# Inverse of the long convolution: plain float32 products become three products of split operands

## The reference, cut to what matters

```python
n = 2 * L                                     # L = 512 tokens
y = jnp.fft.irfft(jnp.fft.rfft(s, n=n, axis=1) * jnp.fft.rfft(g, n=n, axis=0)[None], n=n, axis=1)[:, :L]
y = (y + s * skip.astype(jnp.float32)).astype(u.dtype) * x0
return y @ w_out + b_out
```

## Time and profile before

| | us |
|---|---|
| median of 3 runs (1364.06 to 1364.46) | 1364.25 |
| the profiled execution: its own time | 1364.25 |
| the profiled execution: its span | 1362.4 |
| TensorE busy | 1350.7 (99%) |
| VectorE busy | 993.7 (73%) |
| ScalarE busy | 637.4 (47%) |
| GpSimd busy | 122.0 (9%) |

### The profile page before, as it was taken

One profiled execution on the slowest core, in us unless ns is written; L12 is line 12 of the kernel. 1 busy time (PEld: TensorE's weight loads), 2 busy tenths in 40 slices (PEclk: granted clock), 3 DMA queues, 4 the chain that ended last, 5 costly groups with the idle time before them and its releaser, 6 DMA issues.

```text
span 1362.4 us, 18513 instructions
## 1 busy us (share of the span) xinstructions
PE 1350.7 (99%) x7232; PEld 1142.9 (84%) x7232; DVE 993.7 (73%) x1348; ACT 637.4 (47%) x901; POOL 122.0 (9%) x143
## 2 busy tenths in 40 slices
PE   9999999999999999999999999999999999999997
PEld 7777887888788889888898888878888899889986
DVE  7767788555666997865886786777878689548844
ACT  6546686333444454542564554533344445325532
POOL 1010157000000000000001221024000000000000
PEclk9999999999999999999999999999999999999999
DMA  7222345422112323223232223341223332322321
GB/s 276 98 98 78 125 145 195 156 79 76 63 62 93 113 103 124 94 93 105 99 107 84 102 93 100 107 160 36 93 93 108 108 124 94 124 93 93 109 77 62
DMA packets 28166, 144.50 MB, mean 106 GB/s; under 512 B 3210, under 2 KB 8611, under 8 KB 13496
## 3 DMA queue, kind: packets, MB, share of 16 engines
q1 hardware_dynamic: 24744, 133.97, 28.7%
q0 software_dynamic: 2656, 8.72, 1.8%
q10 hardware_dynamic: 688, 0.73, 0.2%
HBM read 136.84 MB, written 6.30 MB: 105 GB/s over the span
## 4 chain that ended last, share of the span: by engine, by line
PE 94%; DVE 2%; ACT 1%; DMA 1%; issue 1%; SPq 0%; POOL 0%; DVEq 0%; ACTq 0%
PE ps L2198 28%; PE ps L2200 28%; PE ps L2199 28%; PE ps L2614 1%; PE ps L2416 1%; PE ps L2429 1%; PE ps L2564 1%; PE ps L2406 1%; PE ps L2455 1%; PE ps L2802 1%; PE ps L2800 1%; PE ps L2806 1%; PE ps L2456 0%; PE ps L2457 0%; DMA f_out<-f_out_dram 0%
## 5 line engine op out<-in xcount | busy, mean ns | idle before, releaser
L2198 PE MATMUL ps<-opA_hi,w_hi 128*128 128x512 f32 (+1 forms) x944 | 353.6, 375 | 0.7 <-DVE w_lo L1346 0.4
L2200 PE MATMUL ps<-opA_hi,w_lo 128*128 128x512 f32 (+1 forms) x944 | 349.4, 370 | 0.0
L2199 PE MATMUL ps<-opA_lo,w_hi 128*128 128x512 f32 (+1 forms) x944 | 349.1, 370 | 0.0
L1346 DVE TENSOR_TENSOR w_lo<-raw,w_hi 128x2048 fp32r<-128x2048 f32 x112 | 256.5, 2291 | 77.5 <-ACT w_hi L747 76.2
L747 ACT CAST w_hi<-raw 128x2048 fp32r<-128x2048 f32 x111 | 211.6, 1907 | 190.3 <-PE ps L2200 183.7
L2198 PE MATMUL ps<-opB_hi,w_hi 128*128 128x512 f32 (+1 forms) x584 | 226.8, 388 | 1.7 <-DVE opB_lo L1382 1.0
L2199 PE MATMUL ps<-opB_lo,w_hi 128*128 128x512 f32 (+1 forms) x584 | 225.8, 387 | 0.0
L2200 PE MATMUL ps<-opB_hi,w_lo 128*128 128x512 f32 (+1 forms) x584 | 225.8, 387 | 0.0
L2198 PEld LDWEIGHTS ps<-opA_hi,w_hi 128*128 128x128 f32 x944 | 178.2, 189 | 32.4 <-issue 1.7
L2200 PEld LDWEIGHTS ps<-opA_hi,w_lo 128*128 128x128 f32 x944 | 178.0, 189 | 30.5
L2199 PEld LDWEIGHTS ps<-opA_lo,w_hi 128*128 128x128 f32 x944 | 178.2, 189 | 29.2 <-issue 0.2
(11 more groups left out here) (457 smaller groups left out, 2142.7 us busy)
## 6 DMA issues: line engine op xcount, KB each, us to landing
raw<-weights_dram SPq DMA_DIRECT2D x113, 1024.0 KB, 4.9
g_dram<-g_stage POOLq DMA_DIRECT2D x8, 512.0 KB, 3.0
h<-x_t_dram SPq DMA_DIRECT2D x7, 512.0 KB, 7.0
g_spec<-g_dram SPq DMA_DIRECT2D x5, 512.0 KB, 4.1
scores<-g_dram SPq DMA_DIRECT2D x3, 512.0 KB, 5.3
out_dram<-h SPq DMA_DIRECT2D x6, 256.0 KB, 2.3
mem_raw<-mem_t_dram POOLq DMA_DIRECT2D x1, 1024.0 KB, 8.4
c_keys<-c_dram POOLq DMA_DIRECT2D x4, 256.0 KB, 3.7
```

The source lines that it names most:

```text
L1346: V.tensor_tensor(w_lo[:, p, :], raw[:, p, :], w_hi[:, p, :].bitcast(F32), ALU.subtract).then_inc(lo_ready, 1)
L2198: W.matmul(out, w[0], x[0], start=start, stop=False, skip_group_check=mixed)
L2199: W.matmul(out, w[0], x[1], start=False, stop=False, skip_group_check=mixed)
L2200: return W.matmul(out, w[1], x[0], start=False, stop=stop, skip_group_check=mixed)
```

## The change

The inverse works on split operands. The parts of `y_spec` are made per pair of tiles: `spectrum_hi(half, q)` on ScalarE and `spectrum_lo(half, q)` on VectorE, 128x1024 each, the low part in the place of `y_spec` itself, the high part of half 0 in both slots of `raw` and of half 1 in the place of the products `spec`. `inv` is padded to even column counts (258, 256), ScalarE writes zeros into the pads, and it is split once: high parts into `w_hi[1]` and `inv_hi_es`, low parts in the place of `inv`. TensorE makes three passes where it made one float32 product. The Nyquist rows are copies of the parts, both on ScalarE. As `raw` is taken, both output weight pairs are loaded after `inv_done` 4. Their splits move to other places in both orders. The diff, cut:

```diff
@@ SP
-            sp.wait_ge(lo_ready, F_PAIR)
-            sp.dma_start(raw[:, 1, :], a["weights"][in_dram(I_PAIR + 2)]).then_inc(raw_in[1], 16)
...
-            sp.wait_ge(lo_ready, F_PAIR + 1)
-            sp.dma_start(raw[:, 0, :], a["weights"][in_dram(I_PAIR + 1)]).then_inc(raw_in[0], 16)
             for n in range(3, 8):
                 sp.wait_ge(fs_read, n - 2)
                 load_spectrum(n)
+            for p in range(2):
+                sp.wait_ge(inv_done, 4)
+                sp.dma_start(raw[:, p, :], a["weights"][in_dram(I_PAIR + 1 + p)]).then_inc(raw_in[p], 16)
@@ ScalarE
+            def inv_split_hi():
+                act.wait_ge(inv_patched, 4)
+                A.copy(inv_hi[:], inv[:, 0:ES]).then_inc(inv_patched, 1)
+                act.wait_ge(nyq_row_made, 2)
+                A.copy(inv_hi_es[:], inv[:, ES:]).then_inc(hi_ready, 1)
+            def spectrum_hi(half, q):
+                act.wait_ge(spec_sum, 8 * half + 2 * q + 2)
+                if q == 0:
+                    act.wait_ge(row_zero, 2 * half + 2)
+                A.copy(y_hi[half][:, 2 * q:2 * q + 2, :], y_spec[half][:, 2 * q:2 * q + 2, :]).then_inc(y_hi_made, 1)
...
             row_zero_products(0)
+            act.wait_ge(lo_ready, F_PAIR + 1)
+            spectrum_hi(0, 0)
             inv_patch()
...
+            act.wait_ge(chunk_done, 2 * F_PAIR)
+            inv_split_hi()
+            for q in range(1, 4):
+                spectrum_hi(0, q)
             row_zero_products(1)
-            nyquist_hi(0)
-            nyquist_hi(1)
-            split_after(F_PAIR)
-            split_after(I_PAIR)
-            for c in range(KT):
+            nyquist_rows(0)
+            act.wait_ge(spec_sum, 14)
+            spectrum_hi(1, 0)
+            spectrum_hi(1, 1)
+            even_part(0)
+            act.wait_ge(spec_sum, 16)
+            spectrum_hi(1, 2)
+            spectrum_hi(1, 3)
+            nyquist_rows(1)
+            even_part(1)
+            hyena_out_hi(0)
+            for c in range(2, KT):
                 even_part(c)
-                if c:
-                    hyena_out_hi(c - 1)
+                if c == 4:
+                    split_after(F_PAIR)
+                elif c == KT - 1:
+                    split_after(I_PAIR)
+                hyena_out_hi(c - 1)
@@ VectorE
+            def spectrum_lo(half, q):
+                dve.wait_ge(y_hi_made, 4 * half + q + 1)
+                tiles = slice(2 * q, 2 * q + 2)
+                lo_part(y_lo[half][:, tiles, :], y_spec[half][:, tiles, :], y_hi[half][:, tiles, :]).then_inc(y_lo_made, 1)
             for n in range(8):
-                if n == 7:
-                    nyquist_lo(0)
                 spectrum_products(n)
-            nyquist_lo(1)
+                if n in (2, 4):
+                    spectrum_lo(0, n // 2 - 1)
+                elif n == 3:
+                    dve.wait_ge(hi_ready, I_PAIR + 1)
+                    S.link(lo_part(inv_lo[:, EC:OS], inv[:, EC:OS], inv_hi[:, EC:OS]))
+                    S.link(lo_part(inv_lo[:, ES:], inv[:, ES:], inv_hi_es[:]))
+                elif n == 5:
+                    lo_part(inv_lo[:, OS:ES], inv[:, OS:ES], inv_hi[:, OS:ES]).then_inc(lo_ready, 1)
+                elif n == 6:
+                    spectrum_lo(0, 2)
+            spectrum_lo(0, 3)
+            spectrum_lo(1, 0)
+            spectrum_lo(1, 1)
             V.engine_nop().then_inc(bank_read, 4)
             for c in range(KT):
+                hyena_value(c)
+                if c == 0:
+                    spectrum_lo(1, 2)
+                    spectrum_lo(1, 3)
+                    continue
+                if c == 5:
+                    split_after(I_PAIR)
+                hyena_out_lo(c - 1)
                 if c == 4:
                     split_after(F_PAIR)
-                hyena_value(c)
-                if c:
-                    hyena_out_lo(c - 1)
-                if c == 6:
-                    dve.wait_ge(inv_done, 8)
-                    split_after(I_PAIR)
@@ TensorE, inverse(half)
                         if c == 0:
-                            pe.wait_ge(spec_sum, 8 * half + 2 * q + 2)
+                            pe.wait_ge(y_lo_made, Y_LO_BASE + 4 * half + q + 1)
...
+                        if q < 2:
+                            last = passes(bank[:, HALF - 2:T], y_re, columns(EC + q * (HALF + 2), HALF + 2), q == 0, False, mixed=True)
...
+                            passes(bank[:, 0:HALF], y_im, columns(ES + q * HALF, HALF, back=True), False, False, mixed=True)
                         else:
+                            passes(bank[:, 0:HALF], y_re, columns(OC + (q - 2) * HALF, HALF, back=True), False, False, mixed=True)
+                            passes(bank[:, HALF:T], y_im, columns(OS + (q - 2) * HALF, HALF), False, False, mixed=True)
@@ TensorE, before inverse(0)
-            pe.wait_ge(inv_patched, 1)
-            pe.wait_ge(hi_ready, I_PAIR + 1)
+            pair_ready(I_PAIR)
```

More of the change, by code:

```diff
@@ L135, in program @@
         w_lo = at("w_lo", [P, 2, 2 * CHUNK], F32R, 112 * KB)
[L137 removed]
+        inv, inv_lo = at("inv", [P, INV_COLS], F32, 120 * KB), at("inv_lo", [P, INV_COLS], F32R, 120 * KB)
+        inv_hi = at("inv_hi", [P, ES], F32R, 104 * KB)
         y_spec = [at("y_spec0", [P, KT, T], F32, 16 * KB), at("y_spec1", [P, KT, T], F32, 32 * KB)]
[L139 removed]
+        y_lo = [at("y_lo0", [P, KT, T], F32R, 16 * KB), at("y_lo1", [P, KT, T], F32R, 32 * KB)]
+        o = 128 * KB + 32
         vecs = at("vecs", [P, VECS], F32, o); o += 4 * ((VECS + 7) // 8 * 8)
@@ L752, in split_after @@
                     split_hi((g + 2) // 2, g % 2, past_fold=g + 2 > I_PAIR,
-                             used={F_PAIR: (fs_done, 8), I_PAIR: (chunk_done, 2 * F_PAIR)}.get(g))
+                             used={F_PAIR: (fs_done, 8), I_PAIR: (inv_done, 8)}.get(g))
             def root(i, width=T):
@@ L1200, in inv_patch @@
                 act.wait_ge(inv_in, 64)
-                A.activation(inv[0:1, ES:ES + P], ones[0:1, :], ACT.Copy, scale=0.0).then_inc(inv_patched, 1)
-                A.activation(inv[0:1, ES + P:ES + HALF - 1], ones[0:1, 0:P - 1], ACT.Copy, scale=0.0).then_inc(hi_ready, 1)
+                for cols in (slice(EC, OS, HALF + 2), slice(ES, INV_COLS, HALF)):
+                    A.activation(inv[:, cols], ones[:, 0:2], ACT.Copy, scale=0.0).then_inc(inv_patched, 1)
+                A.activation(inv[0:1, ES + 1:ES + 1 + P], ones[0:1, :], ACT.Copy, scale=0.0).then_inc(inv_patched, 1)
+                A.activation(inv[0:1, ES + 1 + P:ES + HALF], ones[0:1, 0:P - 1], ACT.Copy, scale=0.0).then_inc(inv_patched, 1)
+            def inv_split_hi():
[8 more added lines that the diff above has]
+                A.copy(y_hi[half][:, 2 * q:2 * q + 2, :], y_spec[half][:, 2 * q:2 * q + 2, :]).then_inc(y_hi_made, 1)
             def hy_taps(i, p):
@@ L1248, in hyena_out_hi, with nyquist_rows @@
                 A.copy(op_hi[1][:, c, :], hy_val_feat[:, c % 4, :]).then_inc(u_hi, 1)
-            def nyquist_hi(half):
+            def nyquist_rows(half):
                 act.wait_ge(nyq_cleared, 8 + half)
-                act.wait_ge(row_zero, 2 * half + 2)
-                A.copy(y_nyq[half][0:1, :], y_spec[half][0:1, 1, :]).then_inc(y_nyq_hi, 1)
+                act.wait_ge(y_hi_made, 4 * half + 1)
+                A.copy(y_nyq[half][0:1, :], y_hi[half][0:1, 1, :]).then_inc(y_nyq_lo, 1)
+                act.wait_ge(y_lo_made, Y_LO_BASE + 4 * half + 1)
+                A.copy(y_nyq[half][32:33, :], y_lo[half][0:1, 1, :]).then_inc(y_nyq_lo, 1)
             row_zero_products(0)
+            act.wait_ge(lo_ready, F_PAIR + 1)
+            spectrum_hi(0, 0)
             inv_patch()
@@ L2774, in inverse, with columns @@
             def inverse(half):
-                y = y_spec[half]
+                def columns(start, count, back=False):
+                    if back:
+                        own = slice(start - ES + count - 1, start - ES - 1 if start > ES else None, -1)
+                        whole = slice(start + count - 1, start - 1, -1)
+                        return (inv_hi_es[:, own] if start >= ES else inv_hi[:, whole]), inv_lo[:, whole]
+                    return inv_hi[:, start:start + count], inv_lo[:, start:start + count]
                 for c in range(4):
-                    cs = slice(c * P, (c + 1) * P)
                     bank = ps[:, 4 + c, :]
@@ L2783, in inverse @@
                         if c == 0:
-                            pe.wait_ge(spec_sum, 8 * half + 2 * q + 2)
[L2785 to L2797, removed]
-                        else:
[L2799 to L2807, removed]
+                            pe.wait_ge(y_lo_made, Y_LO_BASE + 4 * half + q + 1)
+                        y_re, y_im = ([part[half][:, 2 * q + f, c * P:(c + 1) * P] for part in (y_hi, y_lo)] for f in range(2))
+                        if q < 2:
```

(11 more changed lines are left out.)

16 lines of the change are left out of this document (9 added, 7 removed).

## The result

The changed kernel takes 1369.67 us (1368.45 to 1371.68, 5 runs) against 1364.25 us (1363.96 to 1364.46, 5 runs): ratio 1.004, 95% interval 1.0029 to 1.0051, so slower by 5.4 us. Forecast were 1368.9 and a range of 1364.6 to 1371.6. The profiled execution took 1369.67 us (span 1367.8, 1.87 around it); all rows of after are from it.

The account below looks back on a forecast made before the run. TensorE, busy 99%, was taken as the bound; its 4.6 us saving would be spent waiting for VectorE's low parts, and chunk 2 would start at 969.7 instead of 965.05: 1364.25 + 4.65 = 1368.9 us, range 1364.6 to 1371.6.

Parts of the forecast that it names:

- TensorE's saving: Inverse: three split passes replace each float32 product, 24.0 us instead of 28.60, 4.6 less if nothing makes TensorE wait.
- The first inverse tile: TensorE waits there for low (0,2) to 934.4 and for low (0,3) from 935.2 to 938.05.
- VectorE's stage: VectorE's queue from 914.84 to chunk 2's start at 969.7; under 51 us would show the forecast wrong.
- The port: VectorE's low parts and GpSimd's instructions take turns at SBUF, adding 3.9 us (between 0 and 11).
- ScalarE's copy: Behind tile 5, VectorE idles 3.0 us for slot 1's high copy, queued behind hyena_out_hi(5) and even_part(7).
- TensorE's wait for slot 0: After the inverse ends at 959.95, TensorE waits for slot 0's low part until 961.9.
- the mis-sized term: Start of chunk 2 in hy_out: 969.7 instead of 965.05, the whole forecast difference of +4.65 us.
- The clock: Rival, chance 0.03: TensorE's clock falls in the new gaps, chunk 2's costing up to 2.7 us more: 1371.6.
- The argument from the earlier trace: At the earlier span's end, the clock fell only after TensorE had been nearly idle for over 2 us.
- The tight last low part: hy_out, chunk 0 behind chunks 2 and 3: needs the last low part at 977.25; VectorE has it at 977.1.
- all fits: Rival, chance 0.07: low parts fit VectorE's idle time, so the whole 4.6 us is saved: 1359.7.
- The reason given against it: VectorE's idle time lies early, and the 3.0 us behind tile 5 have no other work.

Follow-up runs that it names:

- no_lo_act: The changed kernel without the eleven low parts of y_spec and inv on VectorE, and with slot 1's high copy ahead of hyena_out_hi(5): 1360.81 us (0.9974).
- lo03_act: act_order with the low part (0,3) ahead of the products of n = 7 on VectorE: 1368.05 us (ratio 1.0023).
- warm_both: warm_chunk2 plus ten unneeded TensorE products in the gap of the first inverse tile: 1368.54 us (ratio 1.003).
- pool_writes: The changed kernel with GpSimd's two additions per n replaced by two clearing writes each, which read nothing: 1366.09 us (ratio 1.0015).
- act_order: The changed kernel with slot 1's high copy on ScalarE moved ahead of hyena_out_hi(5): 1366.63 us (ratio 1.0016).
- warm_chunk2: The changed kernel with eight unneeded TensorE products ahead of chunk 2's wait for slot 1's low part: 1368.42 us (ratio 1.0031).
- best: lo03_act with tile 0 ahead of half 1's low parts, each weight split one step earlier, and ScalarE's copies to match: 1365.95 us (1.001).
- half_split2: act_order with only half 1 of the inverse split, half 0's Nyquist row cleared early, slot 1's weights split ahead of tile 5: 1367.75 us (1.0022).
- no_lo: The changed kernel without the eleven low parts of y_spec and inv on VectorE; TensorE reads the high parts instead: 1362.67 us (ratio 0.999).

## Why the prediction was right

- *TensorE's saving, 4.6 us: right.* Passes stand 0.12 apart, the backward ones too (up to 933.22 every pass starts 0.12 after the last). Without its causes of delay the change gains 3.8 (no_lo_act).
- *The first inverse tile: right.* Idle until low (0,3), as forecast; 0.48 and 2.54 us were measured, of the 2.9 forecast for the long one. In the trace of lo03_act a shorter wait comes back as one for slot 0, and the clock's fall behind it cost nothing (warm_both).
- *VectorE's stage, 54.9 us forecast, 53.9 measured* (914.63 to 968.55). The port took about 3.2 of the 3.9 (pool_writes), ScalarE's copy 2.86 of the 3.0. TensorE's wait for slot 0 was to be 2.0 and hardly exists, since VectorE was nearly a microsecond sooner and TensorE, at the low clock, 0.8 later (960.74 for 959.95). Chunk 2 came 3.5 us late, not 4.65: the mis-sized term. That the port and the copy are what makes it late is shown by pool_writes (2.4 us sooner) and act_order (no wait).
- *The clock: had too small a chance.* It was a rival of 0.03, priced at up to 2.7 us on top. It came in addition to the forecast and cost 1.71 in chunk 2 (1.25 by warm_chunk2). The argument from the earlier trace rows, that the clock falls only after more than 2 us of near idleness, let the gap of 1.83 us through too easily, and the forecast's own gaps of 2.9 and 2.3 us were longer than that. The Trainium skill, "TensorE: Matmul & The Clock Gate", section "Part 1: The HAM clock gate (the "warmup" mystery)", has the return to 1.2 GHz between bursts; the windows from 938 and 970 agree, at 0.51 and 0.50.
- *The tight last low part:* no wait of TensorE behind chunk 2, as forecast. It wasn't tight: VectorE had it at 975.9 (974.47 and 1.46), not 977.1.

That 1369.67 lies so near 1368.9 is thus two errors of opposite sign, 1.15 us too much for VectorE and 1.7 too little for the clock, on a mechanism whose pieces the runs confirm; that the sum is so close is luck. The rival *all fits* falls with the result, and none of the orders tried brought it back. The reason given against it holds: of VectorE's 9.9 idle us of the earlier trace rows 9.2 lie ahead of 940, by the windows of before (910 to 940: 7.73, 6.82 and 6.29 busy of 10 each), and the weights and the hyena output come later.

## What to carry to other kernels

A bound engine can be relieved only as far as the engine that feeds it can still deliver in time: lay out that engine's queue in order up to the need, and don't go by its mean busy share. Look for the copy that stands behind a waiting instruction on a nearly idle engine: here it was worth 3.0 us, more than half the loss, and moving it costs nothing. Count what a new gap of TensorE does to the products behind it, and ask first whether they are on the path.

## What was not expected of the hardware

- The clock fell after gaps of 1.83 to 2.55 us, and in lo03_act and best after one of 1.23 and 1.24 (windows at 0.58 and 0.50). It need not: in pool_writes gaps of 2.55 us ahead of 936.24 and 1.84 ahead of 966.18 left it at 1.00, and so did one of 1.95 in half_split2.
- In the changed kernel the slow passes lasted 3.3 and 3.5 us (938.0 to 941.3, 968.5 to 972.0), in act_order, behind the same gap, 5.3 (937.6 to 942.9). So the price of a fall isn't one number.
- It seems to differ from run to run of one kernel. no_lo has seven runs from 1361.99 to 1363.42 with a mean clock of 0.998 and four from 1364.31 to 1364.75 with 0.997, and the profiled one, of the second group, shows the fall. In five runs each the kernel before spreads over 0.5 us, the changed one over 3.2. But lo03_act has its two groups at nearly the same mean clock (0.997, one run 0.998). That the clock's fall behind a gap is what divides the runs of no_lo is argued from these clocks; only one run of each kernel has a trace.
- A clearing write on GpSimd left VectorE's two-operand instructions at their own length (0.69, 3.48), which an addition does not.
